# Norm sums in column groups, an eighth ring slot, and a reordered merge stage in a two-block network on one core

## The reference, cut to what matters

```
# first network, per layer i (0: stick-breaking attention, 1: dilated attention)
hn = rms_norm(x, gains[i,0]);  m = attention_i(hn) @ w_o
x  = x + rms_norm(m, gains[i,1])
f  = (silu(g) * u) @ w_down, with g, u = causal_conv3(rms_norm(x, gains[i,2]) @ w_up)   # D_FF 2816
x  = x + rms_norm(f, gains[i,3])
# second network, per block i
sh1, sc1, gt1, sh2, sc2, gt2 = silu(c) @ w_ada[i] + b_ada[i]          # 1024 x 6144, also for the context
h  = rmsnorm(x, g1) * (1 + sc1) + sh1;   proj = h @ w_in              # 1024 x 7168
ya = neighbourhood attention;  yb = head_norm(differential attention);  yc = gated MLP
x  = x + gt1 * ((sum over b of sigmoid(gate_b) * (y_b @ w_branch[b])) @ w_out)
h2 = rmsnorm(x, g2) * (1 + sc2) + sh2
x  = x + gt2 * expert_choice_moe(h2)      # 16 experts, 1024 -> 1024 -> 1024, 32 tokens each
out = rmsnorm(x, g_final)
```

## Time and profile before

| | us |
|---|---|
| median of three runs | 2985.76 |
| the profiled execution | 2987.7 |
| its span, first to last instruction | 2985.8 |
| TensorE busy | 2671.9 (89%) |
| VectorE, ScalarE busy | 793.7, 509.5 |
| granted TensorE clock, mean | 0.947 |
| HBM read | 660.67 MB |

### The profile page before, as it was taken

How to read it: one execution, slowest core, us unless ns; L and a number is a source line. 1 busy time by engine, 2 the same in 40 slices (tenths; PEclk the granted TensorE clock), 3 DMA queues, 4 the chain that set the end, 5 groups by cost and what they waited for, 6 DMA issues and landing times.

```text
span 2985.8 us, 30763 instructions
## 1 busy us (share of the span) xinstructions
PE 2671.9 (89%) x13275; PEld 1579.5 (53%) x13275; DVE 793.7 (27%) x1659; ACT 509.5 (17%) x1041; POOL 55.6 (2%) x85
## 2 busy tenths in 40 slices
PE   8899999999999999999988898887999996676665
PEld 6678888478874444444443243334457883232322
DVE  2525411435412453331130011012344312000001
ACT  1620020230021031222031111113021321000001
POOL 1000000000002000000000000001100000000000
PEclk9999999999999999999999999999999997776777
DMA  7645444555465201212139999999422338999995
GB/s 255 212 156 163 162 141 143 206 162 166 156 196 120 85 29 57 71 57 71 57 141 412 421 421 421 420 421 327 123 80 99 127 134 337 420 421 421 421 421 241
DMA packets 201018, 663.80 MB, mean 222 GB/s; under 512 B 13426, under 2 KB 58784, under 8 KB 151604
## 3 DMA queue, kind: packets, MB, share of 16 engines
q1 hardware_dynamic: 192912, 641.90, 56.3%
q0 software_dynamic: 7776, 19.88, 3.0%
q10 hardware_dynamic: 196, 0.06, 0.0%
HBM read 660.67 MB, written 9.57 MB: 224 GB/s over the span
## 4 chain that ended last, share of the span: by engine, by line
PE 69%; DMA 24%; DVE 4%; ACT 3%; issue 1%; ACTq 0%; DVEq 0%
PE ps L471 39%; DMA ring<-in_w_e 24%; PE ps L492 7%; PE ps L1032 6%; PE ps L638 5%; PE ps L518 2%; PE ps L987 1%; PE ps L1013 1%; PE ps L884 1%; PE ps L575 1%; PE ps L906 1%; PE ps L839 1%; PE ps L852 1%; ACT normed L1848 1%; PE ps L827 1%; DMA ring<-in_w_ada 1%
## 5 line engine op out<-in xcount | busy, mean ns | idle before, releaser
L471 PE MATMUL ps<-normed,ring 128*128 128x256 f32 (+1 forms) x3456 | 943.2, 433 | 17.1 <-ACT normed L1848 11.4
L1032 PE MATMUL ps<-ring,arena 128*32 128x256 f32 (+1 forms) x4608 | 641.2, 539 | 210.3 <-DMA ring<-in_w_e 203.4
L471 PEld LDWEIGHTS ps<-normed,ring 128*128 128x128 f32 x3456 | 655.4, 191 | 284.0 <-issue 206.0
L1032 PEld LDWEIGHTS ps<-ring,arena 128*32 128x32 f32 (+1 forms) x4608 | 205.4, 135 | 625.7 <-DMA ring<-in_w_e 323.7
L471 PE MATMUL ps<-arena,ring 128*128 128x256 f32 (+1 forms) x832 | 255.1, 464 | 6.4 <-DVE small L1149 6.4
L492 PE MATMUL ps<-ring,normed 128*128 128x512 f32 x512 | 222.0, 592 | 0.0
L471 PEld LDWEIGHTS ps<-arena,ring 128*128 128x128 f32 x832 | 157.5, 191 | 95.1 <-issue 73.8
L1230 DVE COPY arena<-ps 128x256 f32<-128x256 f32 (+1 forms) x102 | 56.0, 554 | 420.1 <-PE ps L471 176.3
L492 PEld LDWEIGHTS ps<-ring,normed 128*128 128x128 f32 x512 | 96.4, 190 | 117.2 <-issue 117.2
L638 PE MATMUL ps<-arena,ring 128*128 128x256 f32 x704 | 152.3, 379 | 0.0
L638 PEld LDWEIGHTS ps<-arena,ring 128*128 128x128 f32 x704 | 133.8, 190 | 18.2
(11 more groups left out here) (231 smaller groups left out, 1858.3 us busy)
## 6 DMA issues: line engine op xcount, KB each, us to landing
ring<-in_w_e SPq DMA_DIRECT2D x384, 1024.0 KB, 15.4
ring<-in_w_in SPq DMA_DIRECT2D x56, 1024.0 KB, 6.8
ring<-in_w_ada SPq DMA_DIRECT2D x48, 1024.0 KB, 6.1
ring<-in_ffn_w_up SPq DMA_DIRECT2D x88, 512.0 KB, 5.9
ring<-in_ffn_w_down SPq DMA_DIRECT2D x22, 1024.0 KB, 5.1
ring<-in_dil_w_qkv SPq DMA_DIRECT2D x18, 1024.0 KB, 5.1
ring<-in_sb_w_qkv SPq DMA_DIRECT2D x12, 1024.0 KB, 12.6
ring<-in_w_branch SPq DMA_DIRECT2D x12, 1024.0 KB, 7.4
```

What stands on the lines that cost most here:

```text
L471: ins = mm(o[:, 0:n], slots[k // 4][:, k % 4, f * P:(f + 1) * P], src[:, k, 0:n], start=k == 0, stop=k == kts - 1)
L1032: ins = mm(o[w * g:w * g + w, 0:cols], lhs(2 * c + j), slot[:, j, g * cols:(g + 1) * cols], start=c == 0 and j == 0, stop=c == KT // 2 - 1 ...
```

## The change

1. **Sums of squares.** `square_sums` writes four column groups of 32 partitions with 32 columns of `mean`; ScalarE copies the bank to SBUF with scale 1/32 (`PART`, 512 columns); `total_squares` is one matmul with `ones`, and ScalarE's Ln reads its bank. All 13 sums go this way. In `panels_before_norm` the third tile stands between the two matmul steps; elsewhere nothing does.
2. **Ring.** `NSLOT` 8 for 7, and the scratch for dynamic DMA descriptors is set to 8192 bytes.
3. **ADA fold.** Moving side 32 columns instead of 128 per matmul.
4. **Merge stage.** The first two tiles of gate panel 4 run before the four head sums, the other two behind them. ScalarE does these two tanh, Ln of all heads, then Exp of all heads.
5. **Output panels.** `merged_ready` is raised after each half of `MB`; the first tile of the first output panel waits for the first half before `k` = 0 and for the second before `k` = 4.
6. **Places.** `ones` moves into the first constant load (192 KB for 128 KB, the later load shorter by as much); the first norm's squares lie at another place in the arena.

```
-NSLOT = 7
+NSLOT = 8
-            def mean_square(src, n, tiles, m):
+            def square_sums(src, n):
                 o = banks.open("a")
...
-                for k in range(tiles):
+                for k in range(KT):
                     if k % GRP == 0:
                         pe.wait_ge(sq_ready.sem, sq_ready.nth("pe"))
-                    ins = mm(o[:, 0:n], m, src[:, k, 0:n], start=k == 0, stop=k == tiles - 1)
+                    ins = mm(o[32 * (k % 4):32 * (k % 4) + 32, 0:n], mean[:, 0:32], src[:, k, 0:n], start=k < 4, stop=k >= 4)
                 ins.then_inc(banks.filled, 1)
+                return sum(r[-1] == "a" for r in banks.uses)
+
+            def total_squares(n, read):
+                o = banks.open("a")
...
+                pe.wait_ge(banks.freed["a"], read)
+                mm(o[:, 0:n], ones, PART[:, 0:n], start=True, stop=True).then_inc(banks.filled, 1)
+
+            def mean_square(src, n):
+                total_squares(n, square_sums(src, n))
...
                 for step in tiles[0:2]:
                     step()
-                mean_square(squares, S, KT, mean)
-                for step in tiles[2:]:
+                read = square_sums(squares, S)
+                tiles[2]()
+                total_squares(S, read)
+                for step in tiles[3:]:
                     step()
...
-                    ins = mm(o[:, f * P:(f + 1) * P], ada_rows(n)[:, f * P:(f + 1) * P], cst("fold32"), start=True, stop=True)
+                    ins = mm(o[:, f * P:f * P + 32], ada_rows(n)[:, f * P:(f + 1) * P], cst("fold32")[:, 0:32], start=True, stop=True)
...
+                gate_tiles = tiles_T(H, qtok, readers=("a",))
+                for step in gate_tiles[0:2]:
+                    step()
                 pe.wait_ge(sq_ready.sem, sq_ready.nth("pe"))
...
-                gemm_T(1, H, qtok, readers=("a",))
+                for step in gate_tiles[2:]:
+                    step()
...
-                pe.wait_ge(merged_ready.sem, merged_ready.nth("pe"))
-                gemm_T(2, MB, qtok)
+                for step in tiles_T(MB, qtok, halves=merged_ready) + tiles_T(MB, qtok):
+                    step()
...
-                stamp().then_inc(merged_ready.sem, merged_ready.up())
+                    stamp().then_inc(merged_ready.sem, merged_ready.up())
...
+            def total(n):
+                o = banks.take("a")
+                sc.wait_ge(banks.filled, banks.at["a"])
+                se.activation(PART[:, 0:n], o[:, 0:n], ACT.Copy, scale=1.0 / 32).then_inc(banks.freed["a"], banks.free("a"))
+                o = banks.take("a")
+                sc.wait_ge(banks.filled, banks.at["a"])
+                return o[:, 0:n]
...
-                for h in range(DA_HEADS):
+                gate_tile(4, 0)
+                gate_tile(4, 1)
+                heads = [S2[h // 2][:, h % 2, 0:qtok] for h in range(DA_HEADS)]
+                for root in heads:
                     o = banks.take("a")
                     sc.wait_ge(banks.filled, banks.at["a"])
-                    inverse_root(S2[h // 2][:, h % 2, 0:qtok], o[:, 0:qtok], qtok)
+                    se.activation(root, o[:, 0:qtok], ACT.Ln, bias=eps).then_inc(banks.freed["a"], banks.free("a"))
+                sc.wait_ge(banks.freed["a"], banks.frees["a"])
+                for root in heads:
+                    se.activation(root, root, ACT.Exp, scale=-0.5).then_inc(rstd_ready.sem, rstd_ready.up())
...
-    nc = bacc.Bacc("TRN2", target_bir_lowering=False, num_devices=1)
+    nc = bacc.Bacc("TRN2", target_bir_lowering=False, num_devices=1, dynamic_dma_scratch_size=8192)
```

More of the change, by code:

```diff
@@ L57 @@
 C_AT, C_N = {}, 0
-for _name, _w in (("ident", P), ("mean", P), ("mean_head", P), ("ones", P), ("suffix", P), ("rot", P),
+for _name, _w in (("ident", P), ("mean", P), ("ones", P), ("mean_head", P), ("suffix", P), ("rot", P),
                   ("cos", S), ("sin", S), ("sb_keep", 384), ("sb_neg", 384), ("iota", CAP), ("col_neg", GRID_W),
@@ L362, in build @@
         SM = view(22000, 8, S)
-        X_SQ = view(22528, 8, S)
+        X_SQ = view(12288, 8, S)
+        PART = view(24064, 512)
         SBUFS = [view(8192 + 768 * i, 2, 384) for i in range(16)]
@@ L453, in chunks_done, with tiles_T @@
                     freed_at.append(len(banks.uses))
[L455 removed]
+            def tiles_T(src, n, kts=KT, readers=("v",), fresh=False, halves=None):
                 slots = []
@@ L470, in tile @@
                             pe.wait_ge(h_ready.sem, h_ready.nth("pe"))
+                        if halves and f == 0 and k % 4 == 0:
+                            pe.wait_ge(halves.sem, halves.nth("pe"))
                         ins = mm(o[:, 0:n], slots[k // 4][:, k % 4, f * P:(f + 1) * P], src[:, k, 0:n],
@@ L647, in ffn @@
                         chunks_done(1)
-                mean_square(H, S, KT, mean)
+                mean_square(H, S)
                 ada_gap(ADA_BLOCK[i])
@@ L783, in _ @@
                 qtok, qtiles = (S, ST) if last else (2 * S, 2 * ST)
-                mean_square(H, 2 * S, KT, mean)
+                mean_square(H, 2 * S)
                 if last:
@@ L1112, in _ @@
         def _(sp):
-            sp.dma_start(Cb[:, 0:2 * P], a["const_table"][:, 0:2 * P]).then_inc(loads["ident"], 16)
+            sp.dma_start(Cb[:, 0:3 * P], a["const_table"][:, 0:3 * P]).then_inc(loads["ident"], 16)
             sp.dma_start(view(X_STAGE, ST, D), a["x"][0].rearrange("(t p) d -> p t d", p=P)).then_inc(loads["x"], 16)
@@ L1821, in norm @@
                     se.activation(H[:, k:k + GRP, 0:n], src[:, k:k + GRP, 0:n], ACT.Square).then_inc(sq_ready.sem, sq_ready.up())
-                o = banks.take("a")
-                sc.wait_ge(banks.filled, banks.at["a"])
-                inverse_root(rstd[:, 0:n], o[:, 0:n], n)
+                inverse_root(rstd[:, 0:n], total(n), n)
             def gain_and_norm(gain, squares):
@@ L1833, in gain_and_norm @@
                     se.activation(squares[:, k:k + GRP, :], X[:, k:k + GRP, 0:S], ACT.Square).then_inc(sq_ready.sem, sq_ready.up())
-                o = banks.take("a")
-                sc.wait_ge(banks.filled, banks.at["a"])
-                inverse_root(rstd[:, 0:S], o[:, 0:S], S)
+                inverse_root(rstd[:, 0:S], total(S), S)
             def gain_of(i, j):
@@ L2026, in _ @@
                 staged(len(items), (0, da_exp), (LAG, lambda n: pt_copy(n, items[n][1])), fill=fill[4:])
-                for h in range(DA_HEADS):
+                gate_tile(4, 0)
+                gate_tile(4, 1)
+                heads = [S2[h // 2][:, h % 2, 0:qtok] for h in range(DA_HEADS)]
+                for root in heads:
                     o = banks.take("a")
                     sc.wait_ge(banks.filled, banks.at["a"])
-                    inverse_root(S2[h // 2][:, h % 2, 0:qtok], o[:, 0:qtok], qtok)
-                for n in range(4, 6):
-                    for f in range(4):
+                    se.activation(root, o[:, 0:qtok], ACT.Ln, bias=eps).then_inc(banks.freed["a"], banks.free("a"))
+                sc.wait_ge(banks.freed["a"], banks.frees["a"])
+                for root in heads:
+                    se.activation(root, root, ACT.Exp, scale=-0.5).then_inc(rstd_ready.sem, rstd_ready.up())
+                for n, f in ((n, f) for n in (4, 5) for f in range(4)):
+                    if (n, f) > (4, 1):
                         gate_tile(n, f)
@@ L2115, in _ @@
             gp.dma_start(arena[0:33, BUCKET:BUCKET + 1152], a["bucket_table"]).then_inc(loads["bucket"], 16)
-            gp.dma_start(Cb[:, 2 * P:C_N], a["const_table"][:, 2 * P:C_N]).then_inc(loads["consts"], 16)
+            gp.dma_start(Cb[:, 3 * P:C_N], a["const_table"][:, 3 * P:C_N]).then_inc(loads["consts"], 16)
             gp.wait_ge(bias_rows.sem, bias_rows.nth("gp"))
```

4 lines of the change are left out of this document (3 added, 1 removed).

## The result

The changed kernel takes 2952.3 us (median of 4 runs, 2949.8 to 2956.3) against 2986.7 us (4 runs) for the kernel before on the same chip: ratio 0.989, 95% interval 0.988 to 0.990, 34.4 us less. The forecast was 36.7 us less and 2949. The profiled execution is the longest of the four: 2956.3, span 2953.6. Set against the profiled execution of before, its span is 32.2 us shorter.

A forecast was written before the change was run, and what follows sets the result against it. TensorE bounds outside the expert stages, the weight stream inside. 8.5 + 0 + 5.2 + 0.5 + 11.0 + 6.7 + 0 + 5.0 - 0.2 = 36.7 us less, forecast 2949 us, range 2940 to 2962.

The forecast's parts named there:

- the fold: ADA fold at 32 moving columns: weight loads set the pace, so 0 taken; bounds 0 and 5 us gained.
- Eighth slot: Both expert stages: one chunk more in the ring at stream start, 2.5 us each, 5.0 us gained.
- Sums in the panels: Four 256-token sums inside packed panels: 2.13 us saved each by grouped matmuls, 8.5 us together.
- the clock takes part back: Rival, chance 0.20: at the nine awaited sums thinner TensorE work lowers the clock, costing 17.6 us, 2967.
- stretches of clock 0.50 inside packed panels: Sign in the profile after the change that would show the prediction wrong.
- Awaited, 256 tokens: Six 256-token sums awaited behind a gemm: copy and uncovered table load replace the matmuls; 0 taken, bounds -0.4 and +0.2 each.
- Table load behind a copy: Awaited sums: load costs 1.28 us; rival, chance 0.03: twice that, nine chains lose 11.5 us, 2961.
- 512 tokens: Three awaited 512-token sums: Ln 2.85 us behind the last square, gains 1.6, 2.0, 1.6: 5.2 us.
- The 0.5 for the ADA products: Before the first 512-token sum TensorE reaches the ADA products earlier: 0.5 us gained (0 to 0.9).
- the 0.2 for the start: Kernel start: 64 KB more loaded ahead of `x`, 0.2 us lost.
- Head norms and output panels: Merge stage, both blocks: gate tiles cover head-norm waits, 11.0 us; output panels start on half their input, 6.7 us.
- The slower side: Two rivals: expert weight stream at a lower rate (0.04); GpSimd's bias loads stall on the halved scratch (0.01).

The follow-up runs named there:

- experiment 5: Kernel before with only the new sums of squares and the moves they need (128-column fold, seven slots, old merge): 2972.9 us against 2984.5, ratio 0.9966.
- experiment 6: Kernel before with only the branch-merge edits (gate tiles before head norms, all Ln first, half-wise wait of output panels): 2968.2 us against 2985.8, ratio 0.9939.
- experiment 4: Kernel before with only eight ring slots and the halved descriptor scratch: 2978.2 us against 2985.8, ratio 0.9975.
- 2: Kernel before with only the ADA fold narrowed to 32 moving columns: 2990.1 us against 2984.5, ratio 1.0015.
- experiment 9: One chip, side by side: kernel before 2983.6 us, changed kernel 2951.3, with 128-column fold 2947.5, with that fold and VectorE copying the nine awaited partial sums 2945.5.
- experiment 7: Changed kernel with 128-column fold and the old packed sums for the six awaited norms over 256 tokens: 2949.2 us against 2985.8, ratio 0.9876.
- Experiment 8: Changed kernel with 128-column fold and VectorE instead of ScalarE copying the partial sums of the nine awaited norms: 2945.6 us against 2985.8, ratio 0.9866.
- experiment 3: Changed kernel with seven ring slots, small descriptor scratch kept: 2956.8 us, ratio 0.9914 to the kernel before.
- experiments 1: Changed kernel with the ADA fold back at 128 moving columns: 2946.2 us, ratio 0.988 to the kernel before.

## Why the prediction was right, point by point

It lay 3 us under the time, with every part of the right sign but one, the fold. Stretch by stretch, the two profiled executions set side by side (us; a forecast is the sum of the terms that fall into the stretch):

| stretch, by the times of the kernel before | gained | forecast |
|---|---|---|
| start to 1055 | 7.2 | 10.4 |
| to the end of block 0's output panels (1520) | 11.5 | 11.3 |
| to the first gather (1557) | 2.0 | 2.0 |
| to the ADA product behind the first expert stage (2045) | 0.0 | 2.5 |
| norm and first panels of block 1 (to 2084) | 3.1 | 1.6 |
| to the end of block 1's output panels (2458) | 6.7 | 6.4 |
| to the second gather (2482) | 0.2 | 0 |
| to the end | 1.6 | 2.5 |

Together that is 32.2 and 36.7. In the two expert stages the slot's gain and the slow gather's 2.4 and 2.3 us stand against each other. In the first panels of block 1, 1.7 us of the gain is the clock: the same panel matmuls took 13.18 us before and 11.49 after, though no edit touches them.

By the experiments, the four parts (5, 6, 4 and 2) alone give 11.5 + 17.6 + 7.6 - 5.6 = 31.1 us, or 32.2 with the fold at the 4.5 of its ratio; on the chip of experiment 9 the whole gave 32.3, on the first 34.4. The parts add up to within the noise of the medians; nothing is given back between them that runs could tell.

- **Sums in the panels.** 8.5 forecast, 4 x 1.82 = 7.3 by the trace. Mis-sized by the eight matmuls in groups (1.00, not 0.89) and by the tile behind them (3.65 for 3.45). In the profiled execution 2.0 of it went to the clock: the two tiles ahead of the feed-forward sums took 10.16 and 9.91 us, not 9.05. That is not steady: the second execution took 9.04 at both places, and of the two with the fold undone one shows 10.18 at the earlier place and the other 9.03. So the rival "the clock takes part back" came true in a small part, in some executions, where the list of signs has "stretches of clock 0.50 inside packed panels".
- **Awaited, 256 tokens.** 0 forecast. The trace has 0.05 lost each, and experiment 7 no difference. Experiment 8 prices the exposed load: with it back in the shadow of the sum Ln comes at 2.08 us, 0.34 sooner, and only then is the grouped form ahead of the old 2.37. The other 2.08 are the last pair of matmuls, the copy, the closing product and the hand-overs between engines. The sum had Ln at 2.22 with the load exposed, 0.2 short.
- **Table load behind a copy.** 1.28 us, with 0.02 on either side. The drain of about 1380 ns that the Trainium skill gives ("ScalarE: Activation LUTs", "What ACT_TABLE_LOAD costs") is not seen in these rows. At the nine awaited sums it would have been 12.4 us (an estimate from that page), which would have left less than 2 of the 14.0 forecast for the sums; experiment 5 gained 11.5.
- **512 tokens.** 5.2 forecast (1.6, 2.0, 1.6); Ln stands 3.06 us behind the last square in all three (881.22, 1506.75, 2043.75), so 1.4 + 1.8 + 1.4 = 4.6. The sum had 0.03 for each hand-over. The one from ScalarE's last square over TensorE's pair to ScalarE's copy is longer: the copy starts 1.15 us behind the last square, with 0.86 of matmul in it. The 0.5 for the ADA products ahead of the first of the three came as about 0.4 (they start 6.2 us earlier, 5.8 gained so far), and the 0.2 for the start is not seen: the first sum starts at 19.61 to 20.56 us in the kernels with the larger first load and at 19.80 to 20.60 in those without.
- **Head norms and output panels.** 11.0 + 6.7 forecast, 17.6 in experiment 6. In the changed kernel block 0 gained 11.5 between 1055 us and the end of its output panels, and block 1 gained 6.7 up to the end of its output panels, where the sum had 5.43 + 2.59 + 3.3 = 11.3 and 3.03 + 1.7 + 1.7 = 6.4. `y_ready` was no new wait, as reckoned.
- **The fold.** The step that failed. It said "The weights set the pace. I take 0", and of the time of the fold itself that nearly holds: the 192 records of all folds are busy 24.8 us at 32 columns and 26.3 at 128, with 23.0 of weight loads in both. But what the fold does to the clock behind it was not asked. Its own upper bound (5 us) was on the side of a gain; the truth was 3.8 to 5.6 lost. The rival "the clock takes part back" was looked for at the thin sums and came mainly at the thin fold.
- **Eighth slot.** 5.0 forecast, 4.5 (experiment 3) to 7.6 (experiment 4), and 2.2 + 3.1 = 5.3 by the means of the 13 traces: right.
- **The slower side.** The rates are 420 and 411 GB/s, before 420 and 414, and GpSimd is busy 55.6 us as before. Neither rival came.

The larger errors are losses (fold 3.8 or more, panels 1.2, 512 norms 0.6, and the clock in the tiles ahead of the sums in some executions), near 6 us together. What the slot, the output panels and the clock elsewhere gave beyond their forecasts makes up for part of it, and the difference is the 2 to 3 us by which the kernel is slower than forecast. That the total lies so close is therefore partly luck: the fold's loss was not in the sum, and as much again as the total's error was made good by gains that were not in it either.

## What to carry to other kernels

Cutting the moving columns of a matmul whose time its weight load sets saves little (here 1.5 us of busy time in 192 records) and can cost the clock of what comes next (here 3.8 us in all); before such a cut ahead of an idle stretch, look at the granted clock in the work behind it, not only at the duration of the cut instruction. When an engine waits on another for one product, look for the independent tiles that can stand in that wait: this was half of the gain, and its two stretches came out to 0.5 us of their sum. And where work is taken off a chain, see what had been hidden under it: the table load was, and moving the copy to an idle engine hid it again.

## What the runs showed of the hardware

- Ahead of the first gather the narrow and the wide fold keep TensorE busy alike (9.79 and 9.80 us of ten, 84 and 83 records), with the same wait of 2.7 us behind it; yet the clock fell well within that wait in 4 of 4 profiled executions with the one (mean clock 0.69 to 0.79), and with the other it stayed at 1.00 up to the gather in 8 of 9 (0.95 in experiment 6). The page's busy share can't tell them apart. Which property of the stretch decides is not settled: folds of 64 columns, or wide ones only right ahead of the gather, were not tried.
- With the wide fold the clock fell in some executions for 1.5 us of loss and in others not, and two executions of one and the same kernel differ so: 7.82 and 9.35 us for the first gather in experiments 1 and 9, and 9.35 and 5.58 against 7.82 and 4.05 for both in experiments 8 and 9. A single profile can't price such a drop.
- A sum in four column groups takes 1.00 us for eight matmuls of 256 columns and 32 outputs, 3.45 when packed over all columns.
- A table load of 1.28 us straight behind a copy from PSUM cost 1.28 us and no more (0.01 to 0.02 us on either side).
- Half the descriptor scratch (8 KB) left GpSimd's loads (55.6 us busy) and the stream (420 GB/s in the first stage) as they were.
